# ScalarE makes the first tap of a gated feed-forward convolution from the PSUM bank, and copies the halo columns

## What is computed

```python
def causal_dwconv(u, w):
    k, c = w.shape
    return lax.conv_general_dilated(
        u, w[:, None, :].astype(u.dtype), window_strides=(1,), padding=[(k - 1, 0)],
        dimension_numbers=("NWC", "WIO", "NWC"), feature_group_count=c)

def conv_ffn(h, w_up, w_conv, w_down):
    u = causal_dwconv(h @ w_up, w_conv)
    gate, val = jnp.split(u, 2, axis=-1)
    return (jax.nn.silu(gate) * val) @ w_down
...
    h = rms_norm(x, ffn_pre_norm[l])
    y = conv_ffn(h, ffn_w_up[l], ffn_conv_w[l], ffn_w_down[l])
    x = x + rms_norm(y, ffn_post_norm[l])
```

## Time and profile before

| | |
|---|---|
| median of the runs | 2615.87 us |
| span of the profiled execution, first to last instruction | 2608.6 us |
| TensorE matmul busy | 2532.9 us, 97% |
| VectorE busy | 1534.2 us, 59% |
| ScalarE busy | 919.9 us, 35% |
| GpSimd busy | 841.4 us, 32% |
| mean granted TensorE clock | 0.995 of full speed |
| idle of TensorE before a matmul from 1140 us on | 14.3 us |

### The profile page before, as it was taken

How to read it: one execution, slowest core, us unless ns; L and a number is a source line. 1 busy time by engine, 2 the same in 40 slices (tenths; PEclk the granted TensorE clock), 3 DMA queues, 4 the chain that set the end, 5 groups by cost and what they waited for, 6 DMA issues and landing times.

```text
span 2608.6 us, 32631 instructions
## 1 busy us (share of the span) xinstructions
PE 2532.9 (97%) x11713; PEld 2102.9 (81%) x11713; DVE 1534.2 (59%) x2448; ACT 919.9 (35%) x1519; POOL 841.4 (32%) x346
## 2 busy tenths in 40 slices
PE   8999999999999999999999999999999999999997
PEld 7877788888787888887888887888887888878886
DVE  4798867887644533458346287255386264682462
ACT  6433232222344333333333343334334233332332
POOL 6531100000032000044544444444345444445342
PEclk9999999999999999999999999999999999999999
DMA  8895675856777767743532335333335332334331
GB/s 257 284 352 215 216 292 187 305 180 226 267 290 286 283 229 262 255 133 96 179 89 92 99 117 170 105 89 97 98 114 181 94 92 87 105 113 154 89 97 65
DMA packets 313816, 452.62 MB, mean 174 GB/s; under 512 B 12072, under 2 KB 234557, under 8 KB 292669
## 3 DMA queue, kind: packets, MB, share of 16 engines
q1 hardware_dynamic: 305101, 438.56, 49.6%
q10 hardware_dynamic: 8560, 12.06, 1.3%
HBM read 368.78 MB, written 81.79 MB: 173 GB/s over the span
## 4 chain that ended last, share of the span: by engine, by line
PE 90%; DVE 5%; issue 1%; DMA 1%; ACT 1%; SPq 0%; ACTq 0%; DVEq 0%
PE colb L1554 19%; PE colb L1556 18%; PE colb L1555 18%; PE accb L1554 11%; PE accb L1556 11%; PE accb L1555 11%; PE colb L1591 2%; DVE accb L1246 2%; PE accb L1766 1%; DMA raw<-in_xattn_wq 1%; DMA kept<-pair 0%; ACT junk L700 0%; DVE small L1086 0%; DVE small L1087 0%; DVE xh L1093 0%
## 5 line engine op out<-in xcount | busy, mean ns | idle before, releaser
L647 POOL TENSOR_TENSOR pair<-raw,pair 128x1024 fp32r<-128x1024 f32 x339 | 840.5, 2495 | 1739.6 <-ACT pair L679 1729.1
L1554 PE MATMUL colb<-hT,pair 128*128 128x512 f32 x1952 | 764.0, 391 | 17.0 <-issue 14.0
L1556 PE MATMUL colb<-hT,pair 128*128 128x512 f32 x1952 | 760.5, 390 | 0.0
L1555 PE MATMUL colb<-hT,pair 128*128 128x512 f32 x1952 | 760.4, 390 | 0.0
L679 ACT ACTIVATE pair<-raw 128x1024 fp32r<-128x1024 f32 x339 | 355.5, 1053 | 482.5 <-PE accb L1556 277.6
L1554 PE MATMUL accb<-pair,act 128*128 128x512 f32 x1120 | 439.2, 392 | 12.2 <-issue 4.6
L1554 PEld LDWEIGHTS colb<-hT,pair 128*128 128x128 f32 x1952 | 367.0, 188 | 102.1 <-issue 27.1
L1556 PE MATMUL accb<-pair,act 128*128 128x512 f32 x1120 | 436.6, 390 | 0.0
L1555 PE MATMUL accb<-pair,act 128*128 128x512 f32 x1120 | 436.6, 390 | 0.0
L1556 PEld LDWEIGHTS colb<-hT,pair 128*128 128x128 f32 x1952 | 367.0, 188 | 77.1
L1555 PEld LDWEIGHTS colb<-hT,pair 128*128 128x128 f32 x1952 | 367.1, 188 | 74.9
(11 more groups left out here) (164 smaller groups left out, 2416.7 us busy)
## 6 DMA issues: line engine op xcount, KB each, us to landing
pair<-kept SPq DMA_DIRECT2D x123, 1024.0 KB, 4.9
raw<-in_ffn_w_up SPq DMA_DIRECT2D x176, 512.0 KB, 3.8
raw<-in_ffn_w_down SPq DMA_DIRECT2D x176, 256.0 KB, 3.0
kept<-pair SPq DMA_DIRECT2D x41, 1024.0 KB, 8.4
raw<-in_w_in SPq DMA_DIRECT2D x17, 512.0 KB, 8.4
xh<-in_x SPq DMA_DIRECT2D x4, 2048.0 KB, 13.9
xt<-in_x SPq DMA_DIRECT2D x4, 2048.0 KB, 15.6
x_mixed<-xt SPq DMA_DIRECT2D x4, 2048.0 KB, 11.1
```

The source lines that it names most:

```text
L647: nc.gpsimd.tensor_tensor(pair[:, b, 1, :], raw[:, r, :], pair[:, b, 0, :].bitcast(F32), ALU.subtract).then_inc(lo_done, 1)
L1554: nc.tensor.matmul(dst, sh, mh, start=first, stop=False)
L1555: nc.tensor.matmul(dst, sh, ml, start=False, stop=False)
L1556: return nc.tensor.matmul(dst, sl, mh, start=False, stop=last)
```

## The change

ScalarE copies the halo columns in front of the pair (both gate and value, 128 x 2 x 2) before the pair's first `hi`; after copying a bank to `uf` it reads the same bank a second time, scaled by the last tap's weight, and writes the sum's first term to `cv`; the bank is freed after this second read. Before the value's term it waits for `lo_written` of the pair before, since that pair's low part is made from the same half of `cv`. After silu it copies out the halo columns for the next tile. VectorE keeps the four accumulating taps, the multiplication with the gate and `lo_y`; it no longer has the two halo copies and the two multiplications. In all, 88 pairs are changed so.

```diff
+        def conv_at(j, e):
+
+            return cv[:, e, :]
...
                 for q in range(2):
                     for j in range(GF):
                         n = q * GF + j
+                        u = uf[:, j % 2, :, :]
+                        hs = halo.rearrange("p (g f) h -> p g f h", g=2)[:, :, n, :]
+                        if n == 0:
+                            sc.wait_ge(conv_ready, pairs.at(FFN, t, 0) + 1)
+                        nc.scalar.activation(u[:, :, 0:HS], hs, ACT.Copy)
                         for e in range(2):
                             i = q * 3 * GF + 2 * j + e
                             c = q * 2 * GF + 2 * j + e
+                            b = bank_of(FFN, c)
+                            w = par_at["ffn2"] + n + KF * e
                             hi(FFN, t, i + AHEAD)
                             slot_full(sc, FFN, t, i)
-                            nc.scalar.activation(uf[:, j % 2, e, HS:LS], colb[bank_of(FFN, c)][:, :], ACT.Copy)\
-                                .then_inc(col_free[bank_of(FFN, c)], 1)
+                            nc.scalar.activation(u[:, e, HS:LS], colb[b][:, :], ACT.Copy)
+                            if e == 1:
+                                sc.wait_ge(lo_written, los.at(FFN, t, n))
+                            nc.scalar.activation(conv_at(j, e), colb[b][:, :], ACT.Copy, scale=par[:, w:w + 1])\
+                                .then_inc(col_free[b], 1)
                         sc.wait_ge(conv_ready, pairs.at(FFN, t, 1 + n) + 1)
-                        nc.scalar.activation(cv[:, 0, :], cv[:, 0, :], ACT.Silu).then_inc(silu_done, 1)
+                        nc.scalar.activation(cv[:, 0, :], conv_at(j, 0), ACT.Silu).then_inc(silu_done, 1)
+                        nc.scalar.activation(hs, u[:, :, T:LS], ACT.Copy)
                         sc.wait_ge(y_ready, ys.at(FFN, t, n) + 1)
-                        nc.scalar.activation(act[:, 0, j, :], cv[:, 1, :], ACT.Copy).then_inc(hi_written, 1)
+                        nc.scalar.activation(act[:, 0, j, :], conv_at(j, 1), ACT.Copy).then_inc(hi_written, 1)
...
-                step(nc.vector.tensor_copy(u[:, :, 0:HS], hs))
                 freed(FFN, t, q * 2 * GF + 2 * j)
                 freed(FFN, t, q * 2 * GF + 2 * j + 1)
-                settle()
-                for k in (2, 0, 1):
+                for k in range(2):
                     for e in range(2):
-                        base = par_at["ffn2"] if k == 2 else par_at["ffn01"] + k * 2 * KF
-                        w = par[:, base + f + KF * e:base + f + KF * e + 1]
-                        if k == 2:
-                            step(nc.vector.tensor_scalar(cv[:, e, :], u[:, e, k:k + T], w, None, ALU.mult))
+                        at_w = par_at["ffn01"] + k * 2 * KF + n + KF * e
+                        if k:
+                            settle(1)
+                        tap = nc.vector.scalar_tensor_tensor(conv_at(j, e), u[:, e, k:k + T], par[:, at_w:at_w + 1], conv_at(j, e),
+                                                             ALU.mult, ALU.add)
+                        if (k, e) == (1, 1):
+                            tap.then_inc(conv_ready, 1)
                         else:
-                            settle(1)
-                            step(nc.vector.scalar_tensor_tensor(cv[:, e, :], u[:, e, k:k + T], w, cv[:, e, :],
-                                                                ALU.mult, ALU.add))
-                settle()
-                nc.vector.tensor_copy(hs, u[:, :, T:LS]).then_inc(conv_ready, 1)
+                            step(tap)
...
-STEPS_PAIR = 7
-STEPS_PREP, STEPS_MIX, STEPS_MIX_LAST, STEPS_ATTN, STEPS_FFN = 159, 180, 82, 45, 183
+STEPS_PAIR = 3
+STEPS_PREP, STEPS_MIX, STEPS_MIX_LAST, STEPS_ATTN, STEPS_FFN = 159, 180, 82, 45, 95
```

More of the change, by code:

```diff
@@ L1387, in ffn_pair @@
                 q, j = divmod(n, GF)
-                f = GF * q + j
                 u = uf[:, j % 2, :, :]
-                hs = halo.rearrange("p (g f) h -> p g f h", g=2)[:, :, f, :]
-                step(nc.vector.tensor_copy(u[:, :, 0:HS], hs))
                 freed(FFN, t, q * 2 * GF + 2 * j)
                 freed(FFN, t, q * 2 * GF + 2 * j + 1)
-                settle()
-                for k in (2, 0, 1):
+                for k in range(2):
                     for e in range(2):
-                        base = par_at["ffn2"] if k == 2 else par_at["ffn01"] + k * 2 * KF
-                        w = par[:, base + f + KF * e:base + f + KF * e + 1]
-                        if k == 2:
-                            step(nc.vector.tensor_scalar(cv[:, e, :], u[:, e, k:k + T], w, None, ALU.mult))
-                        else:
-                            settle(1)
-                            step(nc.vector.scalar_tensor_tensor(cv[:, e, :], u[:, e, k:k + T], w, cv[:, e, :],
-                                                                ALU.mult, ALU.add))
-                settle()
-                nc.vector.tensor_copy(hs, u[:, :, T:LS]).then_inc(conv_ready, 1)
+                        at_w = par_at["ffn01"] + k * 2 * KF + n + KF * e
[5 more added lines that the diff above has]
+                            tap.then_inc(conv_ready, 1)
+                        else:
+                            step(tap)
                 ve.wait_ge(silu_done, pairs.at(FFN, t, n) + 1)
-                nc.vector.tensor_tensor(cv[:, 1, :], cv[:, 1, :], cv[:, 0, :], ALU.mult).then_inc(y_ready, 1)
-                lo_y(FFN, t, n, act[:, 1, j, :], act[:, 0, j, :], cv[:, 1, :])
+                nc.vector.tensor_tensor(conv_at(j, 1), conv_at(j, 1), cv[:, 0, :], ALU.mult).then_inc(y_ready, 1)
+                lo_y(FFN, t, n, act[:, 1, j, :], act[:, 0, j, :], conv_at(j, 1))
             def attn(p, t):
```

## The result

Four executions of the changed kernel took 2588.36 us at the median (2586.86 to 2596.03), beside four of the kernel before with 2615.86 us. The ratio is 0.9905, with a 95% interval of 0.9890 to 0.9921, so 20.7 to 28.8 us were gained. Forecast were 2595.0 us, a ratio of 0.992, and a range from 2592.5 to 2604. The direction and the mechanism came as said.

What follows compares the result with a forecast made beforehand. TensorE was taken to bound the kernel, waiting 21.3 us on a slow ring of ScalarE, VectorE and GpSimd. Of 21.1 us in slots 1 to 26, 0.2 was kept: 2615.87 - 20.9 = 2595.0 us, range 2592.5 to 2604.

Steps and rivals of the forecast that it cites:

- From the sum to the time: Whole kernel: span 2608.6 less 20.9 us; with the runs' median 7.3 above the span, 2615.87 - 20.9 = 2595.0 us.
- The range's lower end: Whole time: 2592.5 us, from a gain of 21.3 us, loop gaps of 0.26 and 0.48, and 1 us between runs.
- What bounds the kernel: TensorE holds 90% of the span's chain, so ScalarE and VectorE changes return only what TensorE waits for them.
- the 21.1 us in slots 1 to 26: First half of each feed-forward tile: TensorE's late slots lose 21.1 us over four tiles, all of it expected to go.
- The port: VectorE's remaining taps share GpSimd's port, so the first waits for the second subtraction, to 7.1 us in the pair.
- The period of 11.26 us: ScalarE, VectorE and GpSimd passing work in feed-forward pairs with a row operation: 11.26 us a pair instead of 12.07.
- the four end at 7.1 + 2.75: VectorE's four taps start at 7.1 us after ScalarE's rounding starts and end at 9.85 us.
- The margins: Feed-forward tiles: slack before TensorE waits, 2.7 to 4.6 us before; the tightest then 3.3 us against 2.7 us lost.
- The second halves run at TensorE's pace already: Second half of each feed-forward tile: no TensorE waits there, so the time gained in the first halves goes to nothing else.
- half as slow: Rival, feed-forward pairs: only the copy out is saved, period 11.87 us, 10.8 us still lost, 2605.6 us; chance 0.12.
- ScalarE becomes the slow part: Rival, feed-forward pairs: ScalarE's tap and copies at upper bounds give a 12.38 us period, 2624.6 us; chance 0.05.
- Nothing changes: Rival, feed-forward pairs: moved work costs ScalarE what it cost VectorE; period stays 12.07 us, time 2615.9 us; chance 0.05.

Runs made afterwards that it cites:

- before again: The kernel before, without any edit, timed and profiled a second time: 2611.63 us, ratio 0.9995 to the kernel before beside it.
- half subtraction: Kernel before, with GpSimd's feed-forward subtraction made over 512 of each slot's 1024 columns, VectorE and ScalarE unchanged: 2588.55 us, ratio 0.9906.
- triple tap: Changed kernel, with each scaled read of a bank by ScalarE made three times, two into an unread buffer: 2592.56 us, ratio 0.9916 to the kernel before.
- halo copies only: Changed kernel with only the halo copies on ScalarE, VectorE multiplying the last tap again: 2596.84 us, ratio 0.9949 to the kernel before.

## Why the prediction's time was wrong and its mechanism right

- **From the sum to the time**: this step failed, and with it the range. "The median of the runs lies 7.3 above the span" took all of it for what surrounds the span, and so does the section on time and profile before. That part is 1.9 us (2611.37 against 2609.4 in the run of before again). The profiled execution of before had thus taken some 2610.5 us, 5.4 us less than the median it was set beside. 2610.5 - 20.9 = 2589.6 is what the changed kernel's executions give, 2589.8 on average. The median of 2615.9 was itself 2.9 us above the mean of 58 executions, and the first four of the changed kernel (2588.36) lay 1.4 us below its mean.
- **The range's lower end** left 1 us for differences between executions, read off three runs that lay within 2.1 us. They differ by 3 to 4 us (one standard deviation). Eight in ten of them then lie within some 4 to 5 us of their mean, so the lower end stood 3 to 4 us too high for this alone.
- **What bounds the kernel, and the 21.1 us in slots 1 to 26**: right. 27 slots now take 146.88 us, and 21.1 us are gone (21.7 against the second profile of before).
- **The port**: right, and shown by the half subtraction. The taps wait in place of the multiplications, up to 2.87 us for one. The Trainium skill's GPSIMD Engine Reference, Key points, has it that instructions with two SBUF inputs contend with GpSimd; the taps of the changed kernel agree, 4.54 us for four in place of 2.74.
- **The period of 11.26 us**: it measured 11.07 to 11.13. The step "the four end at 7.1 + 2.75" was 0.2 us too long: a tap that was issued early is done some 0.55 us after the release, not 0.74. The tap's length of 0.68 us (0.682) was right. ScalarE's halo copy is 0.19 us long but moves the next start by 0.09 only, not by 0.2; that is not on the ring's path. Without a row operation the period is 10.47 us (forecast 10.6).
- **The margins**: too small. Take the time from the end of a slot's subtraction to the slot's start, less the 0.1 us that a late slot still has. At slot 5 of the four tiles it was 3.4, 4.2, 4.4 and 5.3 us before (taken as 2.7 to 4.6) and is 4.7, 5.2, 5.1 and 5.8 us now (forecast 3.3 to 5.2). I had taken the margins from total losses, in which pairs 9 and 10 weigh as well. At slot 19 of tile 0 3.2 us are left, not 0.6; the shorter period gives 1.2 us of that. At the triple tap's 11.32 us tile 0 did hold only just: its slot 25 had 0.1 us, and slot 26 came 0.08 us late. None of this touched the sum.
- **"The second halves run at TensorE's pace already"**: right for TensorE. But the ring there took 11.16 to 11.38 us a pair before, too long as well; no slot was late because the half began with 6.1 us to spare at slot 38 and ended with 2.6 or more.
- **The rivals**: "half as slow" did not come, though the halo copies alone come near it (11.68 us). "ScalarE becomes the slow part" needs some 2.3 us more a pair than the change adds. "Nothing changes" fell with the slots.

## What to carry to other kernels

When several engines pass work round in a ring, work out the period of the ring against that of the bounding engine; what a slow ring costs is its period less that engine's, times the pairs, less the margin. A change is worth what it takes off that and no more: at 11.68 us 6.6 us were lost, at 11.3 none. An instruction whose mean is three times its free duration is a sign to look at who holds what it needs: here four instructions fewer on VectorE, or half the work on GpSimd with VectorE as it was, gave the same 21 us. And set a forecast against the mean of many executions, not against three, before the sum of a single profile is put on it.

## What the runs showed of the hardware that was not expected

- While VectorE and GpSimd both have instructions waiting for the shared port, they take turns by single instructions: one halo copy or one multiplication (halo copies only) passes between two subtractions. The multiplication ended 0.28 us behind the first subtraction, the next one 0.28 us behind the second. Which instruction takes that turn decided 0.2 us a pair.
- A scaled read of a PSUM bank of 128x512 by ScalarE costs 0.682 us, 0.093 more than the unscaled (0.589). The Trainium skill, ScalarE: Activation LUTs, What ACT_TABLE_LOAD costs, gives 93 ns for an operand that is a pointer; the trace agrees.
- TensorE's granted clock fell to 1.2 GHz for parts of the stages ahead of the feed-forward part (0.83 from 280 to 300 us, 0.96 from 800 to 840 us in the first profile of before), in part at other places in each execution, and the times of the kernel before went with the mean clock (2606.5 us at 0.996, 2618.9 at 0.992).
